# Placing half of the later modulation tiles in the scaled rows' memory and loading expert tiles 1, 7 and 12 at other points

## The chip, the cores and the metric

The kernel runs on one core of a Trainium2 chip. The metric is the device time of one execution in microseconds, as the median of several runs. The weights lie in HBM and are brought in by DMA; no host arithmetic takes part.

## The reference

The program computes a `first_block` and two layers of a `second_block` on 256 rows of width 1024, all in f32. The change touches the first block:

```python
mx = (silu(c) @ w_mod + b_mod)              # 6 x 1024: shifts, scales, gates
hx = modulate(rms_norm(x, norm1_g), sh1, sc1)
p  = hx @ w_in                              # attention, hyena, Fourier branch, gates
m  = sigmoid(ga) * (att @ wb_a) + sigmoid(gh) * (hy @ wb_h) + sigmoid(gf) * (fn @ wb_f)
x  = x + g1 * (m @ w_out)
h2 = modulate(rms_norm(x, norm2_g), sh2, sc2)
# 16 experts, each takes the 32 rows with the highest router weight
logits = h2 @ w_router
a, u = xg @ w_gate[e], xg @ w_up[e]         # 1024 x 2048 each
y = (silu(a) * u) @ w_down[e]               # 2048 x 1024
x = x + g2 * scatter_add(y * top_w)
```

## The kernel before, in words

The program is written out by hand for each engine, and the engines meet at semaphores (`c.name`, each a counter). `wait_ge(c.a1, 3)` waits until the counter `a1` has reached 3. Nothing is reordered: each engine works through its own list.

All loads are issued by SP from one list, `queue`, in the order in which the planning code appends to it (lines 343 to 490). A `Load` waits until the memory it goes to (its `Slot`) has been read for the last time, by the count in `used` of the slot's load before it, or by the slot's `first`. As SP takes the list in order, a load that waits holds back all that stand behind it.

The first block's weights come in tiles of 128 x 2048 f32, 1 MB each:

- `wmod`, the modulation weights, 12 products of two tiles each (`load_mod`, `mod_products`); product n counts `modmm` up to 2n + 2. From product 3 on their two tiles go to the two halves of `ahead` (`halves`).
- `wq`, `why`, `wfn`, `wgt` (12 tiles of gate weights), `wbr` (branch weights, four tiles; below wbr 0 to wbr 3) and `wout` (four tiles) go through `ring`. Most of them are "early" tiles: ACT copies a high part and DVE subtracts it for a low part (`part()`, two halves each, DVE's at line 1421), and PE multiplies in three matmuls (`mm3`, lines 501 to 503). wbr 2 and wbr 3 are used without that (line 867).
- `experts`: 16 experts of 24 tiles (8 gate, 8 up, 8 down), numbered 0 to 383 in `todo`.

PE follows one order: attention with the gate products between its steps, then the merge (for each wbr tile three products, `e = 3 * n + j`, in PSUM banks 4 to 7), then `wout`, the router, and the experts. In the merge DVE multiplies each product with its gate and adds it up (lines 1750 and 1754), which frees the bank (`bv`), and has the low parts of wout 0 and wout 1 between them, after n = 1 and n = 3. Line 1732, a reduce ahead of the merge, counts `a1` to 3; PE's one router matmul with `cd` (a matrix of ones in `middles`) waits for it and counts `rt` to 1 after the merge.

The experts' tiles 0 to 23 (expert 0) go one by one into places that the first block has left: 14 in `wide`, 4 in `once` (`PBT`, two parts of `big`, `T1S`) and the six of `ring`. Each place has the count after which it is free. Later tiles are loaded four at a time (4 MB) into `wide_b`, `ring` and `wide_a`, which lie over these places: `wide_b` over those of tiles 8, 9, 10 and 12. So the first such load of `wide_b` waits until PE has read tile 12. In `gather` and the expert loop (line 963 for gate and up, 998 for down) PE reads the tiles in order.

`XN` holds the normalised rows of x at the start, then the hyena branch's buffers `HP` and `HS` until `hyt` 3, and the scaled rows for the experts after the router. `T1S` holds `T1` and `SS`, sums of the convolutions (until `lz` 2) and of the merge. `middles` holds the constants `cd`, `wr`, gains, rope tables and the gates' biases.

Of the kernel before, what the change touches and what calls it, by code (L numbers as in the profile page):

```python
# [88 lines left out]
def program(nc, D, out):  # L89
    f32 = mybir.dt.float32  # L90
    f32r = mybir.dt.float32r
    ALU = mybir.AluOpType
    ACT = mybir.ActivationFunctionType
    X = mybir.AxisListType.X
    with ExitStack() as ctx:
        names = SIGNALS.split()
        c = namedtuple("Signals", names)(*[Count(ctx.enter_context(nc.semaphore("s_" + n))) for n in names])
# [4 lines left out]
        PS = ctx.enter_context(nc.psum_tensor("PS", [128, 8, 512], f32))  # L102
# [3 lines left out]
        XN = sb("XN", [128, 2, 1024])  # L106
        T2 = sb("T2", [128, 1024])
        T1S = sb("T1S", [128, 2048])
# [10 lines left out]
        ones = sb("ones", [128, 128])  # L119
# [9 lines left out]
        ahead = sb("ahead", [128, 2, 2048])  # L129

        with ExitStack() as first:
# [19 lines left out]
            middles = sa("middles", [128, 2048])  # L151
            with ExitStack() as raw:
                mix = sb("mix", [128, 8, 256], f32, raw)
# [8 lines left out]
            QT = sa("QT", [128, 8, 256])  # L162
# [35 lines left out]
        T1 = T1S[:, 0:1024]  # L198
# [5 lines left out]
        cd = middles[:, 1152:1536].rearrange("p (a b) -> p a b", a=3)  # L204
# [42 lines left out]
        wrS = T2[:, 784:800]  # L247
# [39 lines left out]
        def load_mod(n, places=(None, None)):  # L287
            for kh in range(2):
                load("wmod", 2 * MODS[n] + kh, c.modmm, 2 * n + kh + 1, places[kh])
# [16 lines left out]
        def flat(a):  # L306
            return a.rearrange("p a b -> p (a b)")

        wide = [Slot(*at) for at in (
            (ahead[:, 0, :], c.l_c2T, (c.modmm, 23), 1),  # L310
            (ahead[:, 1, :], c.l_x, (c.modmm, 24), 1),
            (filters[:, 0:2048], c.l_filt, (c.pv, 16), 1),
            (front[:, :], c.l_front, (c.gt, 12)),
            (dft[:, :, :, :].rearrange("p a b c -> p (a b c)"), c.wide0, (c.lc, 3)),
            (flat(XT2[:, :, :]), c.wide1, (c.wo, 8), 9),
            (flat(QT[:, :, :]), c.wide2, (c.br, 12), 9),
            (tables[:, :], c.wide3, (c.br, 6)),
            (HRI[:, :, :, :].rearrange("p a b c -> p (a b c)"), c.wide4, (c.br, 6), 1),
            (middles[:, :], c.l_gain, (c.rt, 1), 1),
            (flat(mix[:, :, :]), c.wide5, (c.wo, 8)),  # L320
            (ATG[:, 0:2048], c.l_ctx, (c.xr, 4), 1),
            (flat(XT[:, :, :]), c.wide6, (c.rt, 3)),
            (flat(XR[:, :, :]), c.l_row, (c.wo, 9)))]
# [2 lines left out]
            (PBT[:, :], c.l_id, (c.lc, 4), 1),  # L326
            (big[:, 1536:3584], c.bias, (c.mix, 7), 4),
            (big[:, 3584:5632], c.l_hyc, (c.mix, 7), 2),
            (T1S[:, :], c.l_hyl, (c.mix, 7), 3))]
        todo = [(name, ex * 8 + k, count, 4 * ex + k // 2 + 1 + (ex == 15 and k > 5) if name == "md"  # L330
                      else 16 * ex + o + k + 1)
                     for ex in range(16) for name, count, o in (("mg", c.gu, 0), ("mu", c.gu, 8), ("md", c.dn, 0))
# [2 lines left out]
        def load_expert(slot, at, n=1):  # L335

            name, i, count, value = todo[at + n - 1]
            row = at % 4 * 2048
            w = Load(D["experts"][at // 4, :, row:row + n * 2048], slot, (count, value))
            queue.append(w)  # L340
            for j in range(n):
                name, i = todo[at + j][0:2]
                ap = w.flat[:, j * 2048:j * 2048 + 2048]
                W[name, i] = Tile(ap.rearrange("p (a b) -> p a b", a=2) if name == "md" else ap, w.landed)
# [23 lines left out]
        const(late[:, :], "late", l_hyl)  # L368
        load_early("wfn", 0, c.fn, 1)
        load_mod(4, halves)  # L370
        for n in range(12):
            load_early("wgt", n, c.gt, n + 1)
            if n == 1:
                load_bias(4)
            if 3 < n < 11:
                load_mod(n + 1, halves)
                if n + 1 in GATE:
                    load_bias(n + 1)
            if n == 8:
                load_expert(wide[2], 2)  # L380
            if n == 10:
                load_expert(wide[4], 8)
        load_expert(once[0], 4)

        for n in range(2):
            load_early("wbr", n, c.br, 3 * n + 3)
        for n in range(2):
            load_expert(wide[n], n)
        for n in range(2, 4):
            load("wbr", n, c.br, 3 * n + 3)  # L390
        load_expert(wide[3], 3)
# [3 lines left out]
            load_expert(slot, at)  # L395
        for i in range(2, 4):
            load_early("wout", i, c.wo, 2 * i + 2)
        for at, slot in ((11, wide[6]), (12, wide[9]), (5, once[1]), (6, once[2]), (7, once[3])):
            load_expert(slot, at)
        for i in range(2):  # L400
            cycle[4 + i].last = early[22 + i]
# [81 lines left out]
        def tensor_program():  # L483
            P = Lane(nc.tensor)
# [384 lines left out]
                    held[b] = [(c.bv, 3 * n + j + 1)]  # L869
            take(3)  # L870
            P.wait_ge(c.a1, 3)
            t.matmul(PS[:, 3, 0:16], cd[:, 2, :], wrS, start=True, stop=True).then_inc(*c.rt.up())
            held[3] = [(c.xtv, 7)]

            def turned(m, h):
# [497 lines left out]
        def vector_program():  # L1373
# [3 lines left out]
            def own(i, count=None):  # L1377

                if count is None:
                    count = c.vec  # L1380
                    i.then_inc(*count.up())
                V.wait_ge(count, count.n)
# [359 lines left out]
            for n in range(4):  # L1742
                o = mix[:, 2 * n:2 * n + 2, :].rearrange("p a b -> p (a b)")
                for j in range(3):
                    if n and j == 1:
                        mix_low(n - 1)
                    e = 3 * n + j
                    V.wait_ge(c.br, e + 1)
                    V.wait_ge(c.sg, 4 * j + n + 1)
                    own(v.tensor_tensor(T1[:, 0:512] if j else o, PS[:, 4 + e % 4, :],  # L1750
                                        big[:, (8 * j + 2 * n) * 256:(8 * j + 2 * n) * 256 + 512],
                                        ALU.mult).then_inc(*c.bv.up()), c.bv)
                    if j:
                        i = v.tensor_tensor(o, o, T1[:, 0:512], ALU.add)
                        if j == 2:
                            own(i.then_inc(*c.mix.up()), c.mix)
                        else:
                            own(i)
                if n in (1, 3):
                    part()  # L1760
# [1039 lines left out]
        def gpsimd_program():  # L2800
            G = Lane(nc.gpsimd)
            g = G.e

            def own(i, count=None):

                if count is None:
                    count = c.pool
                    i.then_inc(*count.up())
                G.wait_ge(count, count.n)

            def rsqrt(col, n, width, source, k=1):

                s, u = stat[:, col:col + n], stat[:, col + 32:col + 32 + n]
                G.wait_ge(source, G.nth(source, k))
                own(g.tensor_scalar(u, s, 1.0 / width, EPS, ALU.mult, ALU.add))
                own(g.tensor_tensor(s, u, mhalf[:, 0:n], ALU.pow).then_inc(*c.powr.up()), c.powr)

            own(g.memset(mhalf[:, :], -0.5))
            rsqrt(0, 2, 1024, c.sq)
            rsqrt(0, 2, 1024, c.sq)  # L2820
            G.wait_ge(c.xtp, 8)
            own(g.memset(HP[:, :, 0:1], 0.0))
            own(g.memset(HP[:, :, 257:258], 0.0).then_inc(*c.pad.up()), c.pad)
            rsqrt(0, 16, 64, c.red)
            rsqrt(16, 8, 64, c.red)
            for m in range(2):
                rsqrt(m, 1, 1024, c.sq)
            G.wait_ge(c.oh, 2)
            for ex in range(16):
                if ex:  # L2830
                    G.wait_ge(c.ow, ex)
                for m in range(2):
                    i = g.tensor_copy(OWR[:, m, :].rearrange("p (a b) -> p a b", a=4),
                                      OW[:, m, ex, :].unsqueeze(1).to_broadcast([128, 4, 32]))
                    if m:
                        own(i.then_inc(*c.rp.up()), c.rp)
                    else:
                        own(i)


            own(g.memset(ones[:, :], 1.0))
            for m in range(2):
                rsqrt(m, 1, 1024, c.sq)
            for m in range(2):
                s, u = stat[:, 2 + m:3 + m], stat[:, 34 + m:35 + m]
                G.wait_ge(c.sq, G.nth(c.sq))
                G.wait_ge(c.r1q, m + 1)
                own(g.tensor_scalar(u, s, rr[:, m, 2:3], EPS, ALU.mult, ALU.add))
                own(g.tensor_tensor(s, u, mhalf[:, 0:1], ALU.pow).then_inc(*c.powr.up()), c.powr)

            def add_normed():
                for m in range(2):
                    rsqrt(m, 1, 1024, c.sq)
                    rsqrt(2 + m, 1, 1024, c.sq)

            for l in range(2):
                for col in range(3):
                    rsqrt(col, 1, 1024, c.sq)
                rsqrt(4, 2, 128, c.sq)
                rsqrt(3, 1, 1024, c.sq)  # L2860
                rsqrt(6, 2, 128, c.sq)
                for n in range(4):
                    rsqrt(8 + n, 1, 512, c.sq)
                add_normed()
                add_normed()
                for col in range(4 if l == 0 else 2):
                    rsqrt(col, 1, 1024, c.sq)
# [185 lines left out]
```

## Time and profile before

| | us |
|---|---|
| median of 3 runs | 2290.27 |
| lowest and highest | 2287.51, 2290.91 |
| the profiled execution, its own time | 2288.81 |
| its span, first to last instruction | 2287.5 |
| PE busy | 1930.9 (84%) |
| DVE busy | 985.1 (43%) |
| ACT busy | 670.3 (29%) |
| DMA, share of 16 engines | 70.8% |

The profiled execution is one run of the program with the hardware profiler on; its instructions and transfers are what the rows below show. "busy" is time in instructions other than waits. A chain of waits follows the end back through whatever released each step.

### The profile page before, as it was taken

To read this page: it belongs to the slowest core of one execution; us is meant where nothing else is said; L and a number is where in the kernel's file an instruction comes from. 1 tells how busy PE (TensorE), PEld (TensorE's weight loads), DVE (VectorE), ACT (ScalarE), POOL (GpSimd) and SP (SyncE) were. 2 spreads that over 40 slices of the span, in tenths; PEclk is the share of its full clock that TensorE was granted. 3 is DMA by queue.
4 is the path that set the end of the run, shared out by engine and by line. 5 is a ranking of instruction groups with operands and counts; after the bars stand their busy time and mean duration, and the time that the engine had idled before them with its cause. 6 is when DMAs were issued, how large, how long until landed. Compare 5 with 4: busy or idle time off the path is not lost.

```text
span 2287.5 us, 28991 instructions
## 1 busy us (share of the span) xinstructions
PE 1930.9 (84%) x12332; PEld 1343.7 (59%) x12332; DVE 985.1 (43%) x1234; ACT 670.3 (29%) x817; POOL 66.9 (3%) x144
## 2 busy tenths in 40 slices
PE   7899998555666556666589999999999999999998
PEld 4777952111111111111137998779998999788997
DVE  4755641000000000000006657875667666876656
ACT  4433420000000000000004444554445444455444
POOL 0000000000000000000001001010000000100000
PEclk9999999878777888777899999999999999999999
DMA  9256799999999999999997564245544555425552
GB/s 391 92 203 237 304 403 430 432 431 431 430 431 431 431 431 431 431 431 430 431 387 273 198 211 152 109 151 186 197 166 175 184 196 178 150 91 179 200 192 86
DMA packets 53489, 647.44 MB, mean 283 GB/s; under 512 B 5936, under 2 KB 6448, under 8 KB 10096
## 3 DMA queue, kind: packets, MB, share of 16 engines
q1 hardware_dynamic: 53360, 645.59, 70.8%
q8 instruction: 97, 1.59, 0.3%
q14 instruction: 32, 0.26, 0.0%
HBM read 644.52 MB, written 1.05 MB: 282 GB/s over the span
## 4 chain that ended last, share of the span: by engine, by line
PE 58%; DMA 30%; DVE 6%; ACT 3%; issue 2%; POOL 1%; SPq 0%; DVEq 0%; ACTq 0%; POOLq 0%
DMA wide_b<-in_experts 29%; PE PS L501 14%; PE PS L502 13%; PE PS L503 13%; PE PS L963 4%; PE PS L998 4%; DVE low L1897 1%; PE PS L519 1%; PE PS L941 1%; PE PS L654 1%; DVE PS L1922 1%; DMA ring<-in_wmod 1%; PE PS L867 1%; PE PS L1275 1%; DVE XR L1961 1%
## 5 line engine op out<-in xcount | busy, mean ns | idle before, releaser
L1897 DVE TENSOR_TENSOR low<-ring,WH 128x2048 fp32r<-128x2048 f32 (+1 forms) x163 | 372.1, 2283 | 180.6 <-ACT WH L2286 177.8
L501 PE MATMUL PS<-XH,WH 128*128 128x256 f32 x1408 | 397.6, 282 | 3.4 <-DVE XL L1929 3.2
L502 PE MATMUL PS<-XL,WH 128*128 128x256 f32 x1408 | 396.0, 281 | 0.0
L503 PE MATMUL PS<-XH,low 128*128 128x256 f32 x1408 | 393.6, 280 | 0.0
L2286 ACT ACTIVATE WH<-ring 128x2048 fp32r<-128x2048 f32 (+1 forms) x164 | 313.2, 1910 | 25.2 <-DMA ring<-in_fg 17.7
L501 PEld LDWEIGHTS PS<-XH,WH 128*128 128x128 f32 x1408 | 265.1, 188 | 6.9 <-issue 5.2
L503 PEld LDWEIGHTS PS<-XH,low 128*128 128x128 f32 x1408 | 268.2, 190 | 0.0
L502 PEld LDWEIGHTS PS<-XL,WH 128*128 128x128 f32 x1408 | 265.2, 188 | 1.4
L1879 DVE TENSOR_TENSOR T1S<-T1S,PS 128x512 f32<-128x512 f32 x16 | 11.0, 688 | 545.8 <-PE PS L963 545.8
L963 PE MATMUL PS<-ring,big 128*32 128x512 f32 x936 | 134.0, 722 | 53.5 <-DMA ring<-in_experts 53.5
L2561 ACT ACTIVATE T1S<-PS 128x512 f32<-128x512 f32 x16 | 9.6, 597 | 542.8 <-PE PS L963 542.8
L963 PE MATMUL PS<-wide_a,big 128*32 128x512 f32 x480 | 84.7, 861 | 78.6 <-DMA wide_a<-in_experts 78.6
L501 PE MATMUL PS<-WH,FH 128*128 128x512 f32 x352 | 139.7, 397 | 0.4 <-DVE FL L2027 0.4
L998 PE MATMUL PS<-wide_b,PBT 128*32 128x512 f32 x480 | 80.2, 828 | 70.2 <-DMA wide_b<-in_experts 70.2
L503 PE MATMUL PS<-WH,FL 128*128 128x512 f32 x352 | 138.6, 394 | 0.0
L502 PE MATMUL PS<-low,FH 128*128 128x512 f32 x352 | 138.6, 394 | 0.0
L1887 DVE TENSOR_TENSOR T1S<-PS,ATG 128x512 f32<-128x512 f32 x32 | 22.1, 692 | 255.4 <-PE PS L998 254.7
L963 PE MATMUL PS<-wide_b,big 128*32 128x512 f32 x480 | 81.5, 831 | 54.2 <-DMA wide_b<-in_experts 54.2
L963 PEld LDWEIGHTS PS<-ring,big 128*32 128x32 f32 x936 | 31.6, 129 | 151.5 <-issue 76.1
L501 PE MATMUL PS<-WH,XH 128*128 128x512 f32 (+1 forms) x256 | 104.6, 409 | 4.3 <-DVE low L1897 3.3
L502 PE MATMUL PS<-low,XH 128*128 128x512 f32 (+1 forms) x256 | 99.6, 389 | 0.0
L963 PEld LDWEIGHTS PS<-wide_a,big 128*32 128x32 f32 x480 | 18.0, 150 | 138.8 <-DMA wide_a<-in_experts 90.7
(445 smaller groups left out, 2827.9 us busy)
## 6 DMA issues: line engine op xcount, KB each, us to landing
wide_b<-in_experts SPq DMA_DIRECT2D x30, 4096.0 KB, 23.7
wide_a<-in_experts SPq DMA_DIRECT2D x29, 4096.0 KB, 23.6
ring<-in_experts SPq DMA_DIRECT2D x28, 4096.0 KB, 24.0
ring<-in_fg SPq DMA_DIRECT2D x44, 1024.0 KB, 5.0
ring<-in_fu SPq DMA_DIRECT2D x44, 1024.0 KB, 5.0
ring<-in_fd SPq DMA_DIRECT2D x44, 1024.0 KB, 4.9
ahead<-in_wmod SPq DMA_DIRECT2D x18, 1024.0 KB, 7.9
ring<-in_wgt SPq DMA_DIRECT2D x12, 1024.0 KB, 4.8
```

The costliest lines, as they stand in the source:

```text
L501: t.matmul(o, l[0], r[0], start=start, stop=False, skip_group_check=True)
L502: t.matmul(o, l[0], r[1], start=False, stop=False, skip_group_check=True)
L503: return t.matmul(o, l[1], r[0], start=False, stop=stop, skip_group_check=True)
L519: i = t.matmul(PS[32 * j:32 * j + 32, b, :], c2s[:, kh * 4 + j, :], w.ap[:, j, :], start=kh == 0, stop=kh == 1, skip_group_check=True)
L654: x = t.matmul(PS[:, 4 + half, m * 256:m * 256 + 256], src[:, k, m * 128:m * 128 + 128], w.ap[:, k, :], start=k == 0, stop=k == 7, skip_gr ...
L867: x = t.matmul(o, w[:, k, s], QT[:, k, :], start=at[0], stop=at[1])
L941: x = t.matmul(PS[:, bank, at:at + 32 * (e1 - e0)], XN[:, m, k * 128:k * 128 + 128], big[:, m * 512 + 32 * e0:m * 512 + 32 * e1], start=m ...
L963: x = t.matmul(PS[32 * j:32 * j + 32, b, :], (XG0[:, k, ex * 32:ex * 32 + 32] if ex < 2 else XG2[:, k, ex * 32 - 64:ex * 32 - 32]), w.ap[: ...
L998: x = t.matmul(PS[32 * j:32 * j + 32, n, :], PT[:, 0, i * 128 + 32 * j:i * 128 + 32 * j + 32], ws[j // 2].ap[:, j % 2, n * 512:n * 512 + 5 ...
L1275: x = t.matmul(PS[:, o + m, h * 64:h * 64 + 64], PT2[:, b, i * w + kt * 128:i * w + kt * 128 + 128], v, start=kt == 0, stop=kt == w // 128 ...
L1897: own(v.tensor_tensor(low[:, w.slot.index, 0:size], w.flat, WH[:, w.slot.index, 0:size].bitcast(f32), ALU.subtract).then_inc(*c.wl.up()), ...
L2286: return a.activation(o, i, ACT.Copy)
```

## The change

Three expert tiles are loaded at other points of SP's list, and what had used their memory is moved.

- Modulation products 5 to 11: the second tile goes to `XN` (slot with semaphore `wide5`, free at `hyt` 3) instead of `ahead[1]`. `ahead[1]` is free at `modmm` 10, and tile 1 is loaded into it right behind product 5's tiles.
- Tile 7 into `T1S` is loaded behind tile 4 (`PBT`), free at `lz` 2 instead of `mix` 7. The merge's products on DVE go through `T2` instead of `T1`.
- Tile 12 into `middles` is loaded between wbr 0 and wbr 1, free at `a1` 3 instead of `rt` 1. PE's router matmul reads `ones` instead of `cd`, and POOL sets `ones` at its start.
- Tile 0 follows wbr 1; tile 1 stood behind it before.

```diff
-            (ahead[:, 1, :], c.l_x, (c.modmm, 24), 1),
+            (ahead[:, 1, :], c.l_x, (c.modmm, 10), 1),
...
-            (flat(QT[:, :, :]), c.wide2, (c.br, 12), 9),
+            (flat(QT[:, :, :]), c.wide2, (c.br, 12), 2),
...
-            (middles[:, :], c.l_gain, (c.rt, 1), 1),
-            (flat(mix[:, :, :]), c.wide5, (c.wo, 8)),
+            (middles[:, :], c.l_gain, (c.a1, 3), 1),
+            (flat(mix[:, :, :]), c.wide5, (c.wo, 8), 7),
...
-            (T1S[:, :], c.l_hyl, (c.mix, 7), 3))]
+            (T1S[:, :], c.l_hyl, (c.lz, 2), 3))]
...
         load_mod(4, halves)
+        halves[1] = [Slot(flat(XN[:, :, :]), c.wide5, (c.hyt, 3))]
         for n in range(12):
             load_early("wgt", n, c.gt, n + 1)
...
             if 3 < n < 11:
                 load_mod(n + 1, halves)
+                if n == 4:
+                    load_expert(wide[1], 1)
...
         load_expert(once[0], 4)
-
+        load_expert(once[3], 7)
         for n in range(2):
             load_early("wbr", n, c.br, 3 * n + 3)
-        for n in range(2):
-            load_expert(wide[n], n)
+            load_expert(*((wide[0], 0) if n else (wide[9], 12)))
...
-        for at, slot in ((11, wide[6]), (12, wide[9]), (5, once[1]), (6, once[2]), (7, once[3])):
+        for at, slot in ((11, wide[6]), (5, once[1]), (6, once[2])):
...
             P.wait_ge(c.a1, 3)
-            t.matmul(PS[:, 3, 0:16], cd[:, 2, :], wrS, start=True, stop=True).then_inc(*c.rt.up())
+            P.wait_ge(c.pool, 2)
+            t.matmul(PS[:, 3, 0:16], ones[:, :], wrS, start=True, stop=True).then_inc(*c.rt.up())
...
-                    own(v.tensor_tensor(T1[:, 0:512] if j else o, PS[:, 4 + e % 4, :],
+                    own(v.tensor_tensor(T2[:, 0:512] if j else o, PS[:, 4 + e % 4, :],
...
-                        i = v.tensor_tensor(o, o, T1[:, 0:512], ALU.add)
+                        i = v.tensor_tensor(o, o, T2[:, 0:512], ALU.add)
...
             own(g.memset(mhalf[:, :], -0.5))
+            own(g.memset(ones[:, :], 1.0))
...
-            own(g.memset(ones[:, :], 1.0))
```

SP's list where the gate weights and the later modulation tiles are loaded, before (each row a load into a memory, with the counter that it waits for):

```order
L2879 DMA ring<-in_wgt 128x2048 [waits s_gt]
L2879 DMA ahead<-in_wmod 128x2048 [waits s_modmm] x2
L2879 DMA middles<-in_bmodg 128x512 [waits s_mod]
L2879 DMA ring<-in_wgt 128x2048 [waits s_gt]
L2879 DMA ahead<-in_wmod 128x2048 [waits s_modmm] x2
```

The same place with the change:

```order
L2882 DMA ring<-in_wgt 128x2048 [waits s_gt]
L2882 DMA ahead<-in_wmod 128x2048 [waits s_modmm]
L2882 DMA XN<-in_wmod 128x2048 [waits s_hyt]
L2882 DMA ahead<-in_experts 128x2048 [waits s_modmm]
L2882 DMA middles<-in_bmodg 128x512 [waits s_mod]
L2882 DMA ring<-in_wgt 128x2048 [waits s_gt]
L2882 DMA ahead<-in_wmod 128x2048 [waits s_modmm]
L2882 DMA XN<-in_wmod 128x2048 [waits s_modmm]
```

The second tile of each product is in XN, and tile 1 stands behind the first such pair.

SP's list from the last gate weights to the second pair of wbr tiles, before:

```order
L2879 DMA ring<-in_wgt 128x2048 [waits s_gt]
L2879 DMA PBT<-in_experts 128x2048 [waits s_lc]
L2879 DMA ring<-in_wbr 128x2048 [waits s_gt] x2
L2879 DMA ahead<-in_experts 128x2048 [waits s_modmm] x2
L2879 DMA ring<-in_wbr 128x2048 [waits s_gt] x2
L2879 DMA front<-in_experts 128x2048
L2879 DMA ring<-in_wout 128x2048 [waits s_br] x2
```

And with the change:

```order
L2882 DMA ring<-in_wgt 128x2048 [waits s_gt]
L2882 DMA PBT<-in_experts 128x2048 [waits s_lc]
L2882 DMA T1S<-in_experts 128x2048 [waits s_lz]
L2882 DMA ring<-in_wbr 128x2048 [waits s_gt]
L2882 DMA middles<-in_experts 128x2048 [waits s_a1]
L2882 DMA ring<-in_wbr 128x2048 [waits s_gt]
L2882 DMA ahead<-in_experts 128x2048 [waits s_modmm]
L2882 DMA ring<-in_wbr 128x2048 [waits s_gt] x2
L2882 DMA front<-in_experts 128x2048
L2882 DMA ring<-in_wout 128x2048 [waits s_br] x2
```

T1S (tile 7) has come ahead of the wbr tiles, middles (tile 12) between wbr 0 and wbr 1 with its wait for a1, and one load of ahead (tile 1) is gone.

## Rows read from the trace of the kernel before

**Rows 1.** The page's 40 slices of the span (57.2 us each): PE, GB/s.
```profile
PE   7899998555666556666589999999999999999998
...
GB/s 391 92 203 237 304 403 430 432 431 431 430 431 431 431 431 431 431 431 430 431 387 273 198 211 152 109 151 186 197 166 175 184 196 178 150 91 179 200 192 86
```
**Rows 2.** The page's chain of waits, by line.
```profile
DMA wide_b<-in_experts 29%; PE PS L501 14%; PE PS L502 13%; PE PS L503 13%; PE PS L963 4%; PE PS L998 4%; DVE low L1897 1%; PE PS L519 1%; PE PS L941 1%; PE PS L654 1%; DVE PS L1922 1%; DMA ring<-in_wmod 1%; PE PS L867 1%; PE PS L1275 1%; DVE XR L1961 1%
```
**Rows 3.** The chain in order of time: start us, us, what.
```profile
320.76 13.91 PE PS L963 x128
...
368.71 18.37 DMA wide_b<-in_experts
```
**Rows 4.** Windows: stretch, its us, busy us of each engine, PEclk, DMA share, GB/s.
```profile
240.00:280.00 40.00, 40.00 (x282) 38.17 (x281) 30.14 (x40) 19.47 (x24) 0.00 (x0) 1.00 0.78 300
...
322.00:325.00 3.00, 3.00 (x32) 0.91 (x28) 1.59 (x3) 0.00 (x0) 0.00 (x0) 1.00 0.90 292
334.00:338.00 4.00, 2.60 (x26) 0.97 (x22) 1.38 (x2) 0.38 (x1) 0.59 (x2) 1.00 1.05 326
338.00:368.00 30.00, 29.02 (x156) 9.09 (x152) 3.85 (x6) 2.17 (x3) 0.00 (x0) 1.00 1.00 428
```
**Rows 5.** Timeline of SP's issues: start us, us, what.
```profile
236.53 0.33 SPq L2879 DMA_DIRECT2D ring<-in_wbr  x1
242.18 0.33 SPq L2879 DMA_DIRECT2D ring<-in_wbr  x1
...
259.24 0.33 SPq L2879 DMA_DIRECT2D ring<-in_wout  x1
...
322.73 0.33 SPq L2879 DMA_DIRECT2D ahead<-in_experts  x1
...
332.19 0.33 SPq L2879 DMA_DIRECT2D wide_b<-in_experts  x1
```
**Rows 6.** Timeline of PE at 332 us.
```profile
331.45 0.61 PE L963 MATMUL PS<-middles,big 128*32 128x512 f32 x4
```
**Rows 7.** Issues at 242.18, 242.56 and 339.08 us: count, KB, us to landing.
```profile
ring<-in_wbr SPq DMA_DIRECT2D x1, 1024.0 KB, 5.0
...
ahead<-in_experts SPq DMA_DIRECT2D x1, 1024.0 KB, 7.1
...
ring<-in_experts SPq DMA_DIRECT2D x1, 4096.0 KB, 18.7
```
**Rows 8.** Timeline of SP's issues, 131 to 143 us.
```profile
131.43 1.19 SPq L2879 DMA_DIRECT2D ahead<-in_wmod  x2
...
142.78 0.33 SPq L2879 DMA_DIRECT2D ring<-in_wgt  x1
```
**Rows 9.** Timeline of ACT: high parts of wbr 0 and wbr 1.
```profile
247.93 2.15 ACT L2286 ACTIVATE low<-ring 128x1024 fp32r<-128x1024 f32 x2 [2.89 <-PE PS L503]
...
254.19 2.15 ACT L2286 ACTIVATE low<-ring 128x1024 fp32r<-128x1024 f32 x2
```
**Rows 10.** Timeline of DVE: the reduce, low parts of wbr 1 and wout 0.
```profile
249.92 0.37 DVE L1732 TENSOR_REDUCE T<-T 128x16 f32<-128x128 f32 x1
...
255.35 2.48 DVE L1421 TENSOR_TENSOR low<-ring,low 128x1024 fp32r<-128x1024 f32 x2 [2.54 <-ACT low L2286]
...
266.54 2.48 DVE L1421 TENSOR_TENSOR low<-ring,low 128x1024 fp32r<-128x1024 f32 x2
```
**Rows 11.** Groups of PE, 253.30 to 264.68 us: one of three alike.
```profile
L501 PE MATMUL PS<-QH,low 128*128 128x256 f32 x32 | 9.0, 281 | 0.0
```
**Rows 12.** Timeline of PE: first matmul after an idle time, in brackets.
```profile
43.50 0.47 PE L501 MATMUL PS<-low,XTH 128*128 128x512 f32 x1 [1.41 <-DVE low L1421]
...
81.86 0.35 PE L501 MATMUL PS<-XTH,low 128*128 128x256 f32 x1 [3.31 <-DVE low L1421]
```
**Rows 13.** Windows behind these idle times, columns as in rows 4.
```profile
83.00:87.00 4.00, 4.00 (x23) 4.00 (x22) 3.77 (x7) 0.00 (x0) 0.00 (x0) 0.57 0.02 4
...
43.50:47.50 4.00, 4.00 (x15) 2.46 (x15) 1.80 (x2) 2.41 (x5) 1.10 (x4) 1.00 1.00 418
```

## The prediction, made before the changed kernel was run

> **What bounds the kernel now.** I read the page's 40 slices first [rows 1]. From the seventh to the twentieth slice (about 340 to 1140 us) DMA moves 430 to 432 GB/s, while PE has idle time; before and after that stretch PE is the busy one. The chain of waits by line [rows 2] agrees: "DMA wide_b<-in_experts" has 29% of the span, more than any PE line. So the middle third ends when the last expert byte has landed, and a megabyte taken out of it is worth 1.0486 MB / 431 GB/s = 2.43 us. That is the promise of such a change: three tiles of 1 MB, 7.3 us.
>
> The next question is where the full stretch begins to count. The chain in order of time [rows 3] gives it: PE reads experts on the chain from 320.76 us, and at 368.71 us the first wait for expert weights appears there (18.37 us). Until then nobody waits for a tile, and every tile that the change hastens (0, 1, 7 and 12, all of expert 0) has been read by that time.
>
> What matters before is whether DMA ever runs dry, since a tile landed sooner helps only if the engines then do something else. The windows [rows 4] show 292 GB/s in 322 to 325 us and 326 in 334 to 338, against 428 in 338 to 368: two holes. The queue's timeline [rows 5] says why: `ahead` is issued at 322.73 us and wide_b at 332.19, and each waits for PE to have read old tiles; the 4 MB of wide_b wait for tile 12, the last read of which ("PS<-middles") begins at 331.45 [rows 6]. From 332.19 on there is backlog: the 4 MB issued at 339.08 take 18.7 us to land [rows 7], where 9.7 are their own. Hence **the end of the expert part is set by the issue at 332.19 us plus the bytes behind it**. What was issued before had nearly landed at 334 and could have landed sooner without moving it. The issue moves only with PE.
>
> **The change part by part.**
>
> *Modulation tiles.* Their second halves go to XN, so tile 1 can stay in ahead[1] after product 10. The waits stay on the same counts but for the first, which is now for hyt 3, long given. The extra megabyte goes out behind the issues at 131.43 us; the next large load is at 142.78 [rows 8]. A load on a queue at rest lands in 5.0 us [rows 7] and each behind it 2.4 to 2.5 later, so three issued by 132.7 end near 142. Nobody is hit. Price 0, and tile 1, sooner by 110 us, gains 0 by the argument above.
>
> *T1S sooner.* The products of the merge write T2 instead of T1S: same instructions, same shapes, 0. The load goes out behind PBT, ahead of wbr 0, issued at 236.53 us [rows 5]. Should it cost wbr 0 a whole megabyte, that would land at 236.5 + 5.0 + 2.4 = 244, and ACT takes it only at 247.93 [rows 9]. Price 0.
>
> *ones.* The matmul with `cd` takes `ones` now, and POOL's memset comes at the start; same shapes, 0.
>
> *Middles sooner.* This is the part that costs. The load (tile 12) now stands between wbr 0 and wbr 1 in SP's queue and waits for a1 3. That count is given by the reduce at line 1732, 249.92 to 250.29 us [rows 10]. SP takes its issues in order, so wbr 1, which went out at 242.18 us [rows 5], cannot go before about 250.8, and in front of it is the megabyte of tile 12. At 242 us the first load took 5.0 us and one issued 0.4 us behind it 7.1 [rows 7]. By these, tile 12 lands at 250.35 + 5.0 = 255.4 and wbr 1 at 250.8 + 7.1 = 257.9.
>
> Who waits for wbr 1? ACT begins its high part at 254.19 us [rows 9], now at 257.9. DVE's low part takes the first half 1.1 us after ACT begins (both halves take ACT 2.15) and is done 2.48 us later: 255.35 to 257.83 before [rows 10], now until 257.9 + 1.1 + 2.5 = 261.5. PE's products with wbr 0 and wbr 1 fill 253.30 to 264.68 us [rows 11]: 96 matmuls, 32 for each of three lines, one in 0.118 us, so wbr 1 is first needed at 253.30 + 48 x 0.118 = 259.0. In the profile before the low part was ready 1.1 us early; now PE stands for 261.5 - 259.0 = **2.5 us**.
>
> What else is behind the waiting issue: ahead, wbr 2, wbr 3 and front, then wout 0, issued at 259.24. Counting 2.45 us each from 257.9 they land at 260.3, 262.8, 265.3, 267.7 and 270.2 (wout 0 before: about 264). wbr 2 is needed when PE comes to it, 264.8 + 2.5 = 267.3 us, and is there. wout 0 holds DVE's low part, which sits in the middle of the merge, until about 270.2 + 1.1 + 2.5 = 273.8, where it was 266.54 to 269.02 [rows 10]; the two products behind it free PSUM banks at 274.6 and at about 276. PE asks for these banks only at about 277.8 and 279.6, since wbr 2 and 3 keep it for 14 us from 267.3. It passes with 3 us in hand. All later work is shifted by 2.5 us alike: PE is busy 40.00 of the 40 us from 240 to 280 [rows 4] and stays on the chain.
>
> *Sum.* Gain of the tiles 0; delay of PE 2.5 us, carried to the issue at 332.19 us, which has nothing in hand, and so to the end: 2288.81 + 2.5 = 2291.3 us for an execution like the profiled one. That one is 1.46 below the median of the three runs (2290.27), so the forecast of a median is 2290.27 + 2.5 = **2292.8 us**, slower by 0.11%. I count 0.2% (4.6 us) as what a measurement of this kernel can tell from no change. The term's bounds: if wbr 1 landed with no load in front of it (250.8 + 5.0), 0.4 us would be left; if a second load in front of it added 2.4, 4.9.
>
> **The rivals.**
>
> *The tiles pay.* If the holes at 323 and 335 us were not holes for the DMA engine that finishes last, each megabyte would come off the end: 3 x 2.43 = 7.3 less the stall of 0 to 2.5, so 2283 to 2285.5 us. For it: the holes are shallow (292 and 326, not 0 GB/s). Against: 9.5 us without an issue before 332.19. Chance 0.05.
>
> *Nothing moves.* The stall is taken up by slack that I don't see: 2290.3. Against: PE's 40.00 of 40 us. Chance 0.12.
>
> *The clock falls in the stall.* After PE had idled 3.31 us, until 81.86, the granted clock was 0.57 in 83 to 87 us, that is half speed (1.2 of 2.4 GHz) for 3.4 of 4 us; after 1.41 us of idling, until 43.50, it stayed at 1.00 [rows 12, 13]. The new stall lies between the two. If the clock falls as at 83 us, half of 3.4 us is lost, 1.7 more: 2294.5. Chance 0.14. The Trainium skill ("TensorE: Matmul & The Clock Gate", What's actually happening) calls the throttled state the default, which activity releases; by that rule this case would be the likelier one, and the trace agrees for the long rest and not for the short.
>
> *wout 0 late as well* (the case on the slower side). Its part sits in DVE's fixed order ahead of the products that free banks for wbr 3. It decides when wout 0 lands after about 273 us instead of 270.2, that is when the burst of loads runs 3 us behind my count. Then PE stands a second time, for 1 to 3 us, and with the clock's 1.7 on top: 2290.3 + 2.5 + 2 + 1.7 = 2296.5. Chance 0.07.
>
> **How the numbers follow.** Forecast 0.62, tiles pay 0.05, nothing 0.12, clock 0.14, wout 0.07. The runs of before spread over 3.4 us, so each case has about 1.5 us to either side. The range takes in the forecast with most of its bounds, nothing and clock: 2289 to 2295.8. Slower by over 0.2% (above 2294.9) is most of wout, under half of clock and a tail of the forecast: 0.16. Faster by over 0.2% (below 2285.7) is tiles pay and little else: 0.06. The rest, 0.78, is within.
>
> **What would show it.** In the changed profile SP issues `middles<-in_experts` at about 250.4 us and the second `ring<-in_wbr` at 250.8; PE has an idle time of 2 to 3 us before its matmuls PS<-QH near 261.5, ended by DVE's low part; wide_b is first issued at about 334.7; the holes ahead of it are wider, and the rate of the full stretch is unchanged. If wide_b's first issue comes at 334.7 and the expert part still ends sooner, my reading of the holes is wrong. If PE does not stand at 259 us, the queue argument is.

## The result and the profile after

| | before | after |
|---|---|---|
| median, 21 runs each | 2290.64 | 2295.62 |
| lowest and highest | 2287.51, 2294.28 | 2289.55, 2300.21 |
| profiled execution, its time | 2288.81 | 2293.76 |
| its span | 2287.5 | 2292.5 |

The ratio of the times, after to before, is 1.0016, with a 95% interval of 1.0011 to 1.0022: the change costs 2.5 to 5.0 us, and 3.7 by the ratio. (The two medians are 4.98 us apart.) 2292.8 us had been forecast, 2.5 us above before, with a range to 2295.8; the median lies 0.2 us below that bound. The sign, the place and the absence of a gain came out as forecast; the size by the ratio is larger, and the 2.5 us lie at the edge of the interval.

The page of the changed kernel: PE and GB/s of the 40 slices, and the chain by line.

```profile
PE   7899998666665666666689999999999999999998
...
GB/s 389 84 219 238 306 370 430 430 431 429 431 432 431 431 430 430 432 430 430 431 384 281 193 203 161 112 140 186 202 171 175 184 193 177 152 88 181 197 193 87
...
DMA wide_b<-in_experts 29%; PE PS L503 14%; PE PS L505 13%; PE PS L504 13%; PE PS L966 4%; PE PS L1001 4%; DMA ahead<-in_wmod 1%; DVE low L1900 1%; PE PS L521 1%; PE PS L944 1%; PE PS L656 1%; DVE PS L1925 1%; PE PS L869 1%; DVE XR L1964 1%; PE PS L1278 1%
```

The full stretch is the same as in [rows 1, 2]: 429 to 432 GB/s in slices 7 to 20, 29% on the chain. The sixth slice fell from 403 to 370 GB/s. That is 1.9 MB less in this slice, where tiles 7 and 12 had been loaded (tile 1 had been loaded in the fifth), and nothing took their place.

The issues of SP behind wbr 0, start us, us, what; wbr 1 is the `ring<-in_wbr` at 252.33.

```profile
251.95 0.33 SPq L2882 DMA_DIRECT2D middles<-in_experts  x1
252.33 0.43 SPq L2882 DMA_DIRECT2D ring<-in_wbr  x1
...
260.87 0.33 SPq L2882 DMA_DIRECT2D ring<-in_wout  x1
```

How long these three took to land (count, KB, us):

```profile
middles<-in_experts SPq DMA_DIRECT2D x1, 1024.0 KB, 4.7
...
ring<-in_wbr SPq DMA_DIRECT2D x1, 1024.0 KB, 6.8
...
ring<-in_wout SPq DMA_DIRECT2D x1, 1024.0 KB, 12.0
```

Who waited, on the chain in order of time (start us, us, what):

```profile
251.55 0.38 DVE T L1735
251.95 0.33 SPq L2882
...
252.33 6.79 DMA ring<-in_wbr
...
259.20 1.07 ACT low L2289
...
260.36 1.24 DVE low L1424
261.62 1.24 DVE low L1424
```

And PE's first matmul after it, in the timeline:

```profile
262.90 0.39 PE L503 MATMUL PS<-QH,low 128*128 128x256 f32 x1 [2.06 <-DVE low L1424]
```

This is the forecast path, link by link: the reduce that counts a1, SP released by it, one megabyte in front of wbr 1, ACT's high part 5.0 us later than in [rows 9] (1.6 of which this execution had lost before), DVE's low part, and 2.06 us in which PE stands. In [rows 4] PE was busy 40.00 of the 40 us from 240 to 280; now, in the windows of the changed kernel (first PE busy, third from the end the granted clock):

```profile
240.00:280.00 40.00, 37.94 (x278) 36.38 (x277) 27.03 (x34) 18.33 (x22) 0.00 (x0) 1.00 0.73 290
```

Then the chain at the experts:

```profile
324.74 13.91 PE PS L966 x128
...
372.68 17.94 DMA wide_b<-in_experts
...
1191.44 13.30 DMA wide_b<-in_experts
```

PE comes to the experts 3.98 us later than in [rows 3] (324.74 against 320.76) and the last load of wide_b for the experts lands at 1204.74 us (1191.44 + 13.30), where it was 1200.94 (1186.26 + 14.68), 3.80 later. Of the 4.95 us between the spans, 1.63 were there at the first product of the merge (254.93 against 253.30), 2.35 came in the merge and the router, -0.18 in the expert part, and 1.15 behind that last load. The 1.63 us were lost before the first load that the change moves: the load of gate weights that stands ahead of it went out at 131.47 us, where it was 129.84. At 83 us and behind the last load of wide_b the granted clock was lower than before. The windows there, after:

```profile
83.00:87.00 4.00, 4.00 (x20) 4.00 (x20) 3.75 (x8) 0.00 (x0) 0.00 (x0) 0.50 0.07 29
...
1204.80:1222.20 17.40, 17.27 (x111) 8.00 (x112) 3.09 (x3) 3.10 (x3) 0.00 (x0) 0.92 1.02 424
```

Before, the clock of the first was 0.57 [rows 13], and the same 111 matmuls behind the last load of wide_b took this:

```profile
1201.00:1217.00 16.00, 15.87 (x111) 7.82 (x112) 2.92 (x3) 3.10 (x3) 0.00 (x0) 1.00 1.02 424
```

The code is the same in both stretches, and the other versions show both pictures, with the delay and without: in the 16 us behind its last load of wide_b the clock was 1.00 in wait_only, which has the delay, and 0.83 in mid_behind, which hasn't (both below). So about 2.8 us of the 4.95 are the luck of these two executions, and 2.2 to 2.35 belong to the change.

### The profile page after: what moved, and what is told of

It reads as the page before. It is cut to its first block, busy times and chain, and to the rows that moved or that the text cites. A ratio compares the mean times of both kernels' runs of the same rounds, so it can differ in the third digit from the quotient of the medians.

```text
span 2292.5 us, 28991 instructions
## 1 busy us (share of the span) xinstructions
PE 1941.2 (85%) x12332; PEld 1346.3 (59%) x12332; DVE 985.3 (43%) x1234; ACT 670.5 (29%) x817; POOL 67.2 (3%) x144
## 4 chain that ended last, share of the span: by engine, by line
PE 59%; DMA 30%; DVE 6%; ACT 2%; issue 1%; POOL 1%; SPq 0%; DVEq 0%; ACTq 0%; POOLq 0%
DMA wide_b<-in_experts 29%; PE PS L503 14%; PE PS L505 13%; PE PS L504 13%; PE PS L966 4%; PE PS L1001 4%; DMA ahead<-in_wmod 1%; DVE low L1900 1%; PE PS L521 1%; PE PS L944 1%; PE PS L656 1%; DVE PS L1925 1%; PE PS L869 1%; DVE XR L1964 1%; PE PS L1278 1%
## 5 line engine op out<-in xcount | busy, mean ns | idle before, releaser
L1001 PE MATMUL PS<-wide_b,PBT 128*32 128x512 f32 x480 | 86.8, 888 | 65.5 <-DMA wide_b<-in_experts 65.5
L1001 PE MATMUL PS<-wide_a,PBT 128*32 128x512 f32 x448 | 70.1, 782 | 38.5 <-DMA wide_a<-in_experts 37.7
```

The costliest lines, as they stand in the source:

```text
L1001: x = t.matmul(PS[32 * j:32 * j + 32, n, :], PT[:, 0, i * 128 + 32 * j:i * 128 + 32 * j + 32], ws[j // 2].ap[:, j % 2, n * 512:n * 512 + 5 ...
```

## The experiments

**One part alone and one part away.** `mid_alone` is the kernel before with only tile 12 moved:

```diff
             load_early("wbr", n, c.br, 3 * n + 3)
+            if n == 0:
+                load_expert(wide[9], 12)
```

(with its `a1` wait and `ones`, as in the change). 

> The kernel before with one part of the change: tile 12 loaded between wbr 0 and wbr 1 behind the wait for a1 (and ones in place of cd). Theory (the queue holds wbr 1 back): wbr 1 lands about 10 us later, PE idles 2.0 to 2.5 us ahead of its first matmul with wbr 1, the first 4 MB issue of wide_b comes that much later against the merge's start, and the median is 2 to 4 us above before, like the whole change (+3.7). Rival (the modulation tiles in XN cost something early on): half of the +3.7 is missing here, +2 or less.

Measured: ratio 1.0020 (1.0011 to 1.0029), median 2293.77. wbr 1 landed at 257.02 us instead of 247.21, and PE waited:

```profile
PE PS L503 <- DVE low L1424: 3.1, 2, 2.0
PE PS L869 <- DVE mix L1753: 0.7, 1, 0.7
```

(waited for: us in all, times, longest). The 2.0 us are the stall ahead of wbr 1. The other two waits, 1.0 and 0.7 us, are on DVE around wout 0, which landed at 273.40 us where it was 264.01. From its first product of the merge to its first expert tile PE needed 71.7 us (252.85 to 324.59), 4.3 more than before, with no fall of the clock between. This one part alone costs what the whole change costs, within the intervals; the modulation tiles and T1S are cleared of it. Its trace is even 2 us slower than the changed kernel's between merge and experts (71.7 against 69.7 us): tile 1 is still in the burst of loads behind the wait, one megabyte more ahead of wout 0, which lands 20.6 us after the merge's start and not 17.9.

`mid_behind` is the changed kernel with that one load behind wbr 1 and tile 0:

```diff
             load_early("wbr", n, c.br, 3 * n + 3)
-            load_expert(*((wide[0], 0) if n else (wide[9], 12)))
+        load_expert(wide[0], 0)
+        load_expert(wide[9], 12)
```

> The changed kernel with tile 12 put behind wbr 1 and tile 0 in the queue; all other parts of the change stay. Theory: no idle time of PE between 250 and 270 us, wbr 1 lands near 247 us, and the median equals before within 1 us: the three tiles earn nothing. Rival 'tiles pay': up to 7.3 us below before. Rival 'XN and the rest cost': 1 to 2 us above before.

Measured: ratio 1.0005 (0.9996 to 1.0014), median 2291.27. PE has no wait from 240 to 300 us:

```profile
240.00:280.00 40.00, 40.00 (x284) 38.20 (x283) 30.16 (x40) 19.82 (x24) 0.00 (x0) 1.00 0.76 299
```

From its first product of the merge to its first expert tile PE needed 67.4 us, as before (253.66 to 321.07 against 253.30 to 320.69). All three tiles are loaded sooner here, and no gain is seen. The wait for a1 is in the queue here too, but behind wbr 1 and tile 0, so wbr 1 doesn't stand behind it.

**Three tiles less.** `skip_three` leaves out the loads of tiles 5, 7 and 12; PE reads tiles 6, 6 and 11 for them, so expert 0's products are made with other weights, and 3 MB are not moved.

```diff
-        for at, slot in ((11, wide[6]), (12, wide[9]), (5, once[1]), (6, once[2]), (7, once[3])):
+        for at, slot in ((11, wide[6]), (6, once[2])):
             load_expert(slot, at)
+        for at, other in ((5, 6), (7, 6), (12, 11)):
+            W[todo[at][0:2]] = W[todo[other][0:2]]
...
         load_expert(fours[0], 28, 4)
+        queue[-1].before.append((c.gu, 13))
```

> The kernel before without the loads of tiles 5, 7 and 12: PE reads tiles 6, 6 and 11 in their place, so 3 MB are left out of expert 0, and the waits for reuse of the places are kept. Theory (the end hangs on the first issue of wide_b at 332 us): the median is that of before within 1 us, wide_b's first issue does not move, and the holes of DMA ahead of it are wider. Rival 'tiles pay' (the DMA stretch starts at 280 us): 3 x 2.43 = 7.3 us faster.

Measured: ratio 0.9998 (0.9989 to 1.0007). The interval excludes 7.3 us (0.9968). The slices of 280 to 320 us, 1 us each, DMA's busy tenths and GB/s, in this kernel:

```profile
DMA  0899999999966696000789996067999999999999
GB/s 0 131 393 418 410 467 410 418 418 459 393 279 115 246 410 287 0 0 0 188 377 410 442 434 270 0 115 270 418 442 442 393 434 467 410 393 442 459 410 393
```

and before:

```profile
DMA  3999999999999999999999999989999999999999
GB/s 164 426 410 434 426 410 426 434 426 418 426 434 426 418 426 426 410 426 426 410 434 426 426 401 410 205 360 410 401 442 434 426 401 451 410 442 418 434 410 434
```

Three megabytes taken out of a stretch in which DMA looks full turn into holes, with 0 GB/s in five of the 40 slices (none before), and the time stays. The first issue of wide_b comes 11.5 us after PE's first expert tile, as before (333.61 and 322.12 us). This is the run that shows why loading tiles sooner could not pay: the stretch up to 322 us is filled by what there is to load, and ends when PE gives memory back.

**The issue at 332 us, sooner and later.** `renumber` changes the places of expert 0's tiles, so that those under wide_b hold 4, 6, 8 and 9:

```diff
-                load_expert(wide[4], 8)
-        load_expert(once[0], 4)
-        for at, slot in ((9, wide[8]), (10, wide[7])):
-        for at, slot in ((11, wide[6]), (12, wide[9]), (5, once[1]), (6, once[2]), (7, once[3])):
+                load_expert(wide[4], 4)
+        load_expert(once[0], 12)
+        for at, slot in ((9, wide[8]), (8, wide[7])):
+        for at, slot in ((11, wide[6]), (6, wide[9]), (5, once[1]), (10, once[2]), (7, once[3])):
```

> The kernel before with expert 0's tiles in other places: those under wide_b hold tiles 4, 6, 8 and 9 instead of 8, 9, 10 and 12 (4 and 12, 6 and 12's place, 10 and 6 change about). Theory: PE has read the last of them three tiles sooner, 3 x 0.87 = 2.6 us, so wide_b's first issue comes 2.6 us sooner, the hole of DMA at 334 to 338 us closes, and the median falls by 1.4 us (the idle time of the engines in it) to 2.6 us. Rival 'tiles pay' or any theory in which the issue at 332 us has slack: no change.

Measured: 0.9996 (0.9988 to 1.0005), median 2288.69. A second time:

> The renumbered kernel before once more: its ratio of 0.9996 (0.9988 to 1.0005) was unclear, while its trace had the last expert bytes 1.5 us sooner against the start of the merge. Theory: 1 to 2 us below before again.

Measured: 0.9994 (0.9985 to 1.0002), median 2289.58. `gate_later` adds a wait to the same issue in the kernel before:

```diff
         load_expert(fours[0], 28, 4)
+        queue[-1].before.append((c.gu, 16))
```

> The kernel before in which the first 4 MB issue of wide_b also waits until PE has read tile 15 (gu 16) instead of tile 12: the mirror of the renumbered kernel. Theory (this issue has nothing in hand and sets the end of the expert part): it comes 3 x 0.87 = 2.6 us later, the last expert bytes land 2.0 to 2.6 us later, and the median is 2 to 2.6 us above before. Rival (the stretch has slack there, or is set by the earlier issues): no change.

Measured: 1.0015 (1.0006 to 1.0024), median 2293.52. The issue in SP's timeline of renumber (start us, us, what), and its time to landing in the DMA groups (count, KB, us):

```profile
329.13 0.33 SPq L2879 DMA_DIRECT2D wide_b<-in_experts  x1
```

```profile
wide_b<-in_experts SPq DMA_DIRECT2D x1, 4096.0 KB, 16.6
```

The same two rows of gate_later:

```profile
337.31 0.33 SPq L2880 DMA_DIRECT2D wide_b<-in_experts  x1
```

```profile
wide_b<-in_experts SPq DMA_DIRECT2D x1, 4096.0 KB, 13.5
```

Counted from PE's first expert tile (320.23 and 323.25 us here, 320.69 before) the issue comes at 8.9, 14.1 and 11.5 us, as planned, and lands at 25.5, 27.6 and 27.4; in mid_behind, whose issue is at 11.5 too, at 26.4, and in renumber_again, at 8.9, at 26.1. So the issue has something in hand after all, 1 to 2 us: 2.6 us later, it lands 0.2 to 1.2 later. The load ahead of it in the queue shows why. Its issue and its time to landing, before:

```profile
324.39 0.33 SPq L2879 DMA_DIRECT2D front<-in_experts  x1
```

```profile
front<-in_experts SPq DMA_DIRECT2D x1, 1024.0 KB, 14.0
```

It landed at 338.4 us, 6.2 us after wide_b had been issued: DMA still had bytes of its own to move when the issue at 332.19 came. (In mid_behind it landed 3.5 us after that issue.) The medians point the way the theory says, gate_later clearly. But gate_later's cost by the ratio, 3.4 us, is more than its trace shows: its last load of wide_b lands 0.7 us later after the first expert tile than before. Where the rest comes from stays open. Renumber's gain is not told from zero in either run; against that stands that in its two traces the last load of wide_b landed 1.6 and 2.9 us sooner after the first expert tile than before.

`best` puts both together, the changed kernel with tile 12 behind wbr 1 and the tiles renumbered.

> The changed kernel with tile 12's load behind wbr 1 and tile 0, and expert 0's tiles renumbered so that the places under wide_b hold 4, 6, 8 and 9 (middles holds 6). Theory: like the renumbered kernel before (its median 1.7 below before), within 1 us, for the tiles loaded sooner earn nothing on top. Rival 'once the gate is gone, the sooner tiles pay': 2 us or more below the renumbered kernel.

Measured: 0.9996 (0.9988 to 1.0005), median 2289.23, as the renumbered kernel. No gain of the sooner tiles on top is seen. In its trace the way from the merge to the experts took 67.7 us (67.4 before). No version beats the kernel before by more than its interval.

**Why 3.7 us and not 2.1.** The changed kernel once more:

> The changed kernel once more, beside the others on this chip. Its 21 runs fell into two heaps (8 from 2289.6 to 2292.6 and 12 from 2295.4 to 2300.2 us). If that is a property of the kernel (the granted clock falls after the 2.06 us of idling in some executions and not in others), both heaps show again; if it was the chip, one does, with the median near 2292.5 to 2293 by the stall of 2.1 us alone.

Measured: 1.0013 (1.0004 to 1.0021), median 2294.13, from 2287.8 to 2297.7, without a gap between two heaps; the heaps did not come again. Its trace has the same path with a longer stall. In its DMA groups wbr 1 took this long to land:

```profile
ring<-in_wbr SPq DMA_DIRECT2D x1, 1024.0 KB, 8.4
```

PE's first matmul behind it, in the timeline:

```profile
264.71 0.39 PE L503 MATMUL PS<-QH,low 128*128 128x256 f32 x1 [3.63 <-DVE low L1424]
```

And the window behind that, in the table of windows (the clock is the third number from the end):

```profile
265.00:269.00 4.00, 4.00 (x23) 4.00 (x23) 3.15 (x5) 3.81 (x7) 0.00 (x0) 0.58 1.01 420
```

wbr 1 landed 8.4 us after its issue, not 6.8; PE stood 3.63 us, and then ran at half speed (1.2 of 2.4 GHz; 0.58 in the window) for 3.4 us. From the first product of the merge to the first expert tile it needed 72.8 us, 5.4 more than before. In the third trace (below) it was 69.6 again, 2.2 more. The Trainium skill ("TensorE: Matmul & The Clock Gate", What's actually happening), by which rest brings the throttled clock, agrees with this trace; with the 2.06 us of the first trace it did not come.

Is the clock what lifts the mean? `filled` puts idle matmuls into the gap:

```diff
             for n in range(4):
+                if n == 1:
+                    turn_over(3, 18)
```

> The changed kernel with 18 idle matmuls (ident on ident, 1.95 us in all) in the place where PE stood for 2.06 us ahead of wbr 1. Theory 'clock falls in the stall': the stall's 2.1 us stay, what lies above them goes: median 2292.5, one heap. Theory 'the stall alone' or any other source of the upper heap: no difference to the changed kernel.

Measured: 1.0024 (1.0016 to 1.0033), median 2296.67, above the changed kernel. I had mis-sized the filler: in f32 each is two instructions.

```profile
L500 PE MATMUL PS<-base 128*128 128x128 f32 x36 | 4.2, 275 | 0.0
```

The 18 took 4.2 us and were themselves a longer stall, so this run says nothing on the clock. With nine, beside the changed kernel on the same chip:

> The run before this one of its kind had 18 idle matmuls that took 4.2 us, two times what I had counted, so it lengthened the stall. Here there are 9, which by that row take 2.1 us, as long as the stall in the first trace of the changed kernel. Theory 'the clock falls in some executions': in those in which wbr 1 lands late PE now idles 1.5 us and no longer 3.6, and its clock stays; the mean comes out 0.5 to 1 us below that of the changed kernel. Rival 'only the landing of wbr 1 varies': no difference.

> The changed kernel a third time, beside the two above. Its two traces differ: wbr 1 landed 6.8 us after its issue with 2.06 us of idling in one, 8.4 us after it with 3.63 us of idling and a fall of the clock in the other. Theory: a median 3 to 4 us above before again, and one of these two pictures in the trace.

Measured: filled_nine 1.0020 (1.0011 to 1.0029), median 2295.26, from 2290.05 to 2298.18; third 1.0019 (1.0009 to 1.0028), median 2294.76, from 2289.42 to 2299.99. No difference is seen, but a share of 0.5 to 1 us, as expected, is less than these intervals (2 us to either side) can show, so the question stays open. Third's trace has the first picture: 6.9 us to land, 2.15 us of idling, no fall. So the fall occurs; that it lifts the mean is neither shown nor excluded.

**The wait or the megabyte?** `wait_only` keeps the wait in front of wbr 1 and puts tile 12 behind it:

```diff
             load_early("wbr", n, c.br, 3 * n + 3)
-            load_expert(*((wide[0], 0) if n else (wide[9], 12)))
+            if n:
+                queue[-1].before.append((c.a1, 3))
+        load_expert(wide[9], 12)
+        load_expert(wide[0], 0)
```

> The changed kernel with wbr 1 still held back until a1 is 3, but tile 12 behind it, so the wait stays and the megabyte in front goes. Theory (the stall is wait plus megabyte): wbr 1 is issued at about 251 to 252 us and lands 4.7 to 5.0 us later, ACT begins its part about 1 us late instead of 4, DVE's 1.1 us in hand take that up, PE idles under 0.5 us, and the median is within 1.5 us of before. Rival 'the wait alone is the cost': the stall of 2 us and the median of the changed kernel stay.

Measured: 1.0019 (1.0010 to 1.0028), median 2293.32: no cheaper than the changed kernel, where a median within 1.5 us of before had been expected. wbr 1 landed 4.7 us after its issue, the stall ahead of it is gone as expected, and PE came to wbr 2 exactly as before (11.5 us after the merge's start). From the merge's start to the experts PE needed 69.7 us, 2.3 more than before. Two other waits stand in its place, at 278.65 and 288.97 us (PE's list of waits, as for mid_alone):

```profile
PE PS L506 <- DVE low L1427: 1.0, 1, 1.0
PE PS L872 <- DVE mix L1756: 0.8, 1, 0.8
```

These are waits on DVE, held up by wout 0, which landed at 274.91 us behind six other loads. So the rival "wout 0 late as well" is real, but it adds only what the first stall has not yet hidden. In the changed kernel wout 0 lands 17.9 us after the merge's start, PE has stood 2.1 us for wbr 1, and the waits around wout 0 are absent. Here it lands at 18.3 us without that stall, and they cost 1.8. In mid_alone it lands at 20.6 us, and they cost 1.7 on top of a stall of 2.0. The wait for a1 ahead of wbr 1 is enough by itself, since the other loads for the merge come in one burst behind it. The 2.3 us are less than the ratio's 4.3 (2.3 to 6.4), and by the landing of its last load of wide_b only 0.7 of them are left; this trace doesn't show the rest.

## Why the prediction was right, and where not

- *What bounds the kernel; tiles in a stretch that looks full earn nothing.* Right, shown by skip_three (3 MB less, ratio 0.9998) and mid_behind (1.0005). Two readings on the way were slips without effect: tile 0 is not hastened (issued at 242.56 us before, 252.80 after), and modmm 10, after which tile 1 may be loaded, is product 4.
- *Modulation tiles, tile 1, T1S, ones: 0.* Right within mid_behind's interval of -0.9 to +3.2 us; mid_alone carries the whole cost without them.
- *Middles sooner holds wbr 1 back.* Right in each link. "Tile 12 at 255.4 and wbr 1 at 257.9" were, with 1.63 us of earlier offset, to be 257.0 and 259.5; they were 256.64 and 259.11. The stall, forecast at 2.5, was 2.06 us, and 2.15 in the third trace, but 3.63 in the second: 2.6 on average. What failed is the bound that only 0.4 us would be left if wbr 1 landed with no load in front of it. In wait_only it did, and the cost stayed, 2.3 us of it by the first expert tile, with the two waits around wout 0 in the place of the stall.
- *The clock falls in the stall* was given 0.14 and 1.7 us. It occurred in one trace of three. Its price there was about as forecast (5.4 us in all against 3.63 of idling), but it came with the longer stall, and the filler could not show whether it lifts the mean.
- *wout 0 late as well.* Its place was right. In the changed kernel wout 0 landed at 272.83 us, 271.2 less the 1.63 us of offset, and did no harm, as the condition (after 273) says. In mid_alone it landed past 273 and cost 1.7 us, as the rival says. The condition was too strict for a PE without the first stall (wait_only).
- *"It has nothing in hand"*, said of the issue at 332.19 us: too strong. By gate_later's landing it has 1 to 2 us. The "9.5 us without an issue before 332.19" were a misreading, too: `front` went out at 324.39, 7.8 us before, and was still landing. PE's delay shifted the issues alike, but it was not carried whole to the end, as the sum had it. From PE's first expert tile to the landing of the last load of wide_b it took 879.9 to 880.7 us in the traces of before, mid_behind and skip_three, and 880.1, 878.5 and 879.3 in the three of the changed kernel.
- *The sum.* Forecast 2.5, measured 3.7 (2.5 to 5.0). Traces with 2.2, 2.35 and 5.4 us between merge and experts have a mean of 3.3: 2.6 of stall, as forecast, and a fall of the clock in one of three, which the sum left out. I had taken the first landing time at hand (7.1 us for a load behind another) as fixed, and 8.4 us occurs. But by the landing of the last load of wide_b, counted from the merge's start, the three are only 2.2, 3.7 and 1.2 us later than before, 2.3 on average, which is the forecast and not the 3.7. What the executions without a trace add stays open, and so does why wbr 1 lands late in some; that the forecast's 2.5 lies within the interval is in part luck. The wider spread of the changed kernel (2289.6 to 2300.2) fits a stall that varies, but was not traced run by run.

## What to carry to other kernels

A DMA stretch that looks full is worth shortening only from the point where someone waits for its last byte; ahead of that, look for the issue that waits for memory to come free and ask how much is in hand there. Moving a load forward in a queue taken in order moves its wait forward too: the price is the lateness of the first load behind it that has a reader without slack, here 10 us of lateness for wbr 1 against 8 us in hand (7 us before ACT took it, 1.1 us between DVE's part and PE). And a stall that is taken away can uncover the one that it was hiding, so take one away and look for the next.

## What was not expected

- The time from issue to landing of the same load behind the same neighbour was 6.8, 6.9 and 8.4 us in three traces of one kernel, and 6.8, 6.8 and 6.9 in mid_alone, filled and filled_nine, which have the same two loads. A spread of 1.6 us is nearly as large as the effect studied.
- Taking 3 MB out of a run of loads that moved 410 to 430 GB/s left 0 GB/s in five of 40 slices of 1 us and did not move the end.
- Code that is the same in all kernels differed by several microseconds between traces: PE's first context product (PS<-HRI) began at 52.2 to 57.5 us over the 14 traces. Single spans cannot carry an argument on 2 us here; distances between two events in one trace can.
